# The first stage of a two-block transformer kernel: weights of the modulation added up by whole rows, rows turned ahead of them, the affine step on two engines

## The chip, the cores and the metric

The kernel runs on 1 core of one Trainium2 chip. The metric is the device time of one execution in microseconds (us), taken as the median of several runs. Engines are named as the profile names them: PE (matrix products and transposes), DVE (VectorE), ACT (ScalarE), POOL (GpSimd), SP (SyncE, which here only issues the weight loads).

## The reference, cut to what matters

Two blocks of two layers each over x of 256 rows and 1024 columns, in fp32. The change lies in the entry of the layers of the first block, `hybrid_layer`, where a vector `c` of 1024 numbers modulates the rows:

```python
mod = silu(c) @ w_ada[l] + b_ada[l]        # 1024 x 3072; thirds: shift, scale, gate
u = rms_norm(x, norm_g[l]) * (1 + scale) + shift
proj = u @ w_in[l]                          # z, qb, kb, vb, gates ...
...
x = x + gate * (out @ w_out[l])
```

Everything behind it (attention of three kinds, the feed-forward parts of the second block) is untouched.

## The kernel before, in words

**Weights.** All weights come through one stream. `plan` is a list of chunks of 512 KB or less. SP (`sp`, L2169 to L2178) loads them in the order of `plan` into six buffers `raw`; the load of chunk c waits until chunk c-6 has been used up. A chunk of an ordinary weight is split by ACT into a high part `wh` and by DVE into a remainder `wl` (`split` in both engines), and every product on PE is three matmuls: high by high, high by low, low by high. The chunks of `w_ada` take another way: DVE multiplies each row of 512 columns by one number of silu(c) per partition and adds it to an accumulator `acc` of 512 columns (`weigh`, L1335 to L1352). Such a chunk is two row blocks of 512 columns (kq of 4), so one tile of 512 columns takes four chunks, one multiplication and seven multiply-adds. Then `turn_row` lets PE add over the partitions with a column of ones (four matmuls of 128 columns), and DVE adds `b_ada` into `mod`.

**The start of the program.** PE, ACT, DVE and POOL each follow a list written out by hand; a wait holds all that is behind it on its engine. ACT issues the loads of the identity, of eight short vectors (`rows`, c first), of the constants and of x, in this order, and only then computes the tanh of silu(c), which needs its table loaded. POOL issues ten loads of vectors spread over all partitions (`bc`), the loads of the relative bias and the positions, and twelve tiny loads (`cg`), before its first power, which makes 1/sqrt of the mean square. DVE adds up the tiles (0,0), (0,2), (0,1), (0,3) of `w_ada` of layer 0, sixteen chunks in all. After ten chunks comes `rows_norm`: ACT squares the rows of x, POOL gives the factor, DVE scales them into `xn`. PE turns `xn` into columns only after the last tile of `w_ada` has been turned, since its list has them in that order.

**The affine step** (DVE L1620 to L1636, ACT L1004 to L1014). For each of the eight column blocks of 256 numbers: DVE scales and shifts the turned block out of PSUM into `xtmp` (one of the two halves of `dg`), ACT rounds it into `xt_h`, DVE subtracts for `xt_l`. Behind the eight blocks the first product z begins (`gemm`, chunks of 416 columns), and each engine then splits the chunks that are due: the first six chunks behind the sixteen are w_in, w_in, w_ada, w_in, w_ada, w_in. Layer 1 has the same step with its squares, factor, scaling and turning all behind the end of layer 0.

The names to follow are `first_tiles`, `ada`, `turn_row`, `rows_norm`, `weigh`, `to_xt(("x", l) ...)`, `xtmp` and `rot` (the next of PSUM banks 4 to 6).

Of the kernel before, what the change touches and what calls it, by code (L numbers as in the profile page):

```python
# [246 lines left out]
def build(nc, d, out, ctx):  # L247
# [47 lines left out]
    xtmp = [dg[:, 0:256], dg[:, 256:512]]  # L295
# [74 lines left out]
    first_tiles = [(0, j) for j in (0, 2, 1, 3)]  # L370
    side_tiles = {(0, 0): [(1, 0), (1, 1), (1, 2), (0, 4), (0, 5)], (0, 1): [(1, 3)], (1, 0): [(1, 4), (1, 5)], (1, 1): []}
    ada_tiles = first_tiles + [x for k in sorted(side_tiles) for x in side_tiles[k]]
    ada_no = {x: i for i, x in enumerate(ada_tiles)}

    def chunk_view(buf, c):
        kk, n = plan[c][1:3]
        return buf[:, 0:kk * n].rearrange("p (k n) -> p k n", n=n)

# [57 lines left out]
    def pe(e):  # L436
# [68 lines left out]
        def to_xt(s, src, nch, ready, by="xl"):  # L505

            for c in range(0, nch, 2):
                m = min(2, nch - c)
                b = rot(by, s, c + m - 1)
# [77 lines left out]
        def ada(tiles):  # L587
            for i, (l, j) in enumerate(tiles):
                wv = d["w_ada"][l].rearrange("(c p) n -> p c n", p=128)
                for kq in range(4):  # L590
                    if len(plan) == c_no[0]:
                        plan.append((wv[:, 2 * kq:2 * kq + 2, j * 512:j * 512 + 512], 2, 512, None, None, (l, j, kq)))
# [9 lines left out]
        def turn_row(l, j):  # L602
# [5 lines left out]
            w.wait_ge(*at("cst"))  # L608
            for f in range(4):
                last = mm(b[:, f:f + 1], acc[ada_no[l, j] % 2][:, f * 128:f * 128 + 128], ones_col, True, True)  # L610
            last.then_inc(*up("turn", l, j))

# [7 lines left out]
        first = ada(first_tiles)  # L620
        for _ in range(5):
            next(first)
# [3 lines left out]
        for _ in range(15):  # L626
            next(first)

        ps, pts = Ring(pb1), Ring(pt1)
        for l in range(NL):  # L630
            win = d["w_in"][l]
            to_xt(("x", l), lambda c, t: xn[:, t, c * 128:c * 128 + 128], 8, lambda c, t: [("xn", l, t)], by="xm")
# [168 lines left out]
    def act(e):  # L801
# [183 lines left out]
        first = ada(first_tiles)  # L985
        for _ in range(5):
            next(first)
        e.dma_start(mq[0:32, 0, 0:512], d["consts"][0:32, C_OH:C_END]).then_inc(*landed("oh"))
        rot()

        def rows_norm(l, ready):
            for t in range(2):
                w.wait_ge(*at(*ready(t)))
                old_read(XT)
                ac_(xn[:, t, :], h[:, t, :], ACT.Square,
                    accum_out=stat(1, "rn", l, t)).then_inc(*up("rsq", l, t))

        for _ in range(7):
            next(first)
# [293 lines left out]
    def dve(e):  # L1293
# [325 lines left out]
        for l in range(NL):  # L1619
# [3 lines left out]
            if l:  # L1623
                rows_norm(l)
# [609 lines left out]
```

## Time and profile before

| what | us |
|---|---|
| median of 3 runs (1692.60 to 1696.33) | 1695.83 |
| the profiled execution, its own time | 1694.23 |
| span of the profiled execution | 1692.4 |
| mean granted clock of TensorE | 0.988 |

The time of an execution is 1.8 us more than the span between its first and last instruction. A time of a row is counted from the start of the span. The number after x is how often a group was executed. A timeline's row gives the start and the time on the engine, for one instruction or several alike, and in brackets how long the engine stood idle before it and what ended that. A row of ACTq, SPq or POOL with DMA_DIRECT2D is the issue of a load, not its transfer.

### The profile page before, as it was taken

Reading aid. Unit: us, or ns where it says so; the run is one execution under the profiler, and the core shown is the slowest. Engines: PE = TensorE matmul, PEld = TensorE weight load, DVE = VectorE, ACT = ScalarE, POOL = GpSimd, SP = SyncE. Lnnn points to the kernel's source line nnn. Section 1 sums busy time; section 2 is a strip of 40 time slices with the busy share of each in tenths; the row PEclk is TensorE's granted clock in tenths of the full one; section 3 lists DMA queues with packets and bytes.
Section 4 is the critical chain, followed back from the end, with each engine's and each line's share of the span. In section 5 each row is a group of like instructions: output and inputs, shape, how many; then the busy total and the mean of one; then the engine's idle time right before and its main releaser. Section 6 shows DMA issues by size and latency. Waiting matters only on the chain.

```text
span 1692.4 us, 21793 instructions
## 1 busy us (share of the span) xinstructions
PE 1600.2 (95%) x7796; PEld 1318.4 (78%) x7796; DVE 1067.8 (63%) x1792; ACT 855.9 (51%) x1487; POOL 123.9 (7%) x157
## 2 busy tenths in 40 slices
PE   1679989999999999999999999999999999999998
PEld 1567778778888778878788887888878787788886
DVE  5778577666565646567666556565555567675653
ACT  0346536645444565555454445444455655464442
POOL 3011002100000200002100000000020001200000
PEclk9989989999999999999999999999999999999999
DMA  9565257435555664455565556555582454656552
GB/s 286 199 233 191 74 188 237 132 113 185 188 183 192 160 188 120 136 150 156 187 208 170 194 188 191 186 176 193 174 222 79 130 174 125 205 187 191 178 190 75
DMA packets 155336, 293.27 MB, mean 173 GB/s; under 512 B 10214, under 2 KB 23316, under 8 KB 155228
## 3 DMA queue, kind: packets, MB, share of 16 engines
q1 hardware_dynamic: 149312, 276.60, 50.7%
q0 software_dynamic: 4800, 12.29, 3.1%
q10 hardware_dynamic: 1116, 2.99, 0.5%
q8 instruction: 62, 1.02, 0.2%
q14 instruction: 46, 0.38, 0.1%
HBM read 290.77 MB, written 1.06 MB: 172 GB/s over the span
## 4 chain that ended last, share of the span: by engine, by line
PE 79%; DVE 8%; DMA 5%; ACT 3%; issue 2%; POOL 1%; SPq 0%; DVEq 0%; POOLq 0%; ACTq 0%
PE pb L444 75%; PE pb L448 4%; DMA raw<-in_w_in 3%; DVE wl L1312 2%; DVE acc L1309 1%; DMA raw<-in_w_ada 1%; POOL st L2074 1%; ACT wh L814 1%; DVE xt_l L1309 1%; ACT xt_h L814 1%; DVE dg L1306 0%; DVE h L1309 0%; ACT pb L814 0%; DVE xt_l L1312 0%; DVE pb L1315 0%
## 5 line engine op out<-in xcount | busy, mean ns | idle before, releaser
L814 ACT ACTIVATE wh<-raw 128x1024 fp32r<-128x1024 f32 (+1 forms) x484 | 505.9, 1051 | 454.0 <-PE pb L444 391.5
L1312 DVE TENSOR_TENSOR wl<-raw,wh 128x1024 fp32r<-128x1024 f32 (+1 forms) x484 | 581.4, 1219 | 208.7 <-ACT wh L814 204.6
L444 PE MATMUL pb<-wh,xt_h 128*128 128x512 f32 (+2 forms) x1536 | 593.0, 386 | 12.0 <-ACT wh L814 9.9
L444 PE MATMUL pb<-wl,xt_h 128*128 128x512 f32 (+2 forms) x1536 | 584.8, 381 | 11.9 <-DVE wl L1312 11.8
L444 PE MATMUL pb<-wh,xt_l 128*128 128x512 f32 (+2 forms) x1536 | 585.8, 381 | 1.9 <-DVE xt_l L1309 1.7
L444 PEld LDWEIGHTS pb<-wh,xt_h 128*128 128x128 f32 x1536 | 291.8, 190 | 68.4 <-ACT xt_h L814 10.8
L444 PEld LDWEIGHTS pb<-wl,xt_h 128*128 128x128 f32 x1536 | 292.0, 190 | 64.0 <-DVE wl L1312 13.7
L444 PEld LDWEIGHTS pb<-wh,xt_l 128*128 128x128 f32 x1536 | 291.4, 190 | 62.1 <-DVE xt_l L1309 8.5
L444 PE MATMUL pb<-wh,big_h 128*128 128x512 f32 x352 | 138.7, 394 | 0.0
L444 PE MATMUL pb<-wl,big_h 128*128 128x512 f32 x352 | 138.6, 394 | 0.0
L2074 POOL TENSOR_TENSOR st<-st,cols 128x1 f32<-128x1 f32 (+2 forms) x56 | 53.0, 952 | 1146.6 <-DVE st L1309 759.4
L444 PE MATMUL pb<-wh,big_l 128*128 128x512 f32 x352 | 136.7, 388 | 0.0
L444 PEld LDWEIGHTS pb<-wh,big_h 128*128 128x128 f32 x352 | 66.1, 188 | 15.1
L444 PEld LDWEIGHTS pb<-wh,big_l 128*128 128x128 f32 x352 | 66.1, 188 | 14.8
L444 PEld LDWEIGHTS pb<-wl,big_h 128*128 128x128 f32 x352 | 66.2, 188 | 13.0
L814 ACT ACTIVATE p<-p,st 128x256 f32<-128x256 f32 x96 | 48.1, 502 | 50.6 <-DVE st L1315 50.5
L1309 DVE SCALAR_TENSOR_TENSOR sgt<-ti,pb 128x512 f32<-128x512 f32 (+1 forms) x48 | 30.8, 643 | 59.8 <-ACT ti L814 59.4
L1309 DVE SCALAR_TENSOR_TENSOR hid<-pb,few,sgt 128x512 f32<-128x512 f32 (+1 forms) x48 | 33.9, 707 | 54.4 <-PE pb L444 54.4
L1309 DVE SCALAR_TENSOR_TENSOR acc<-raw,st,acc 128x512 f32<-128x512 f32 x84 | 63.0, 750 | 8.0 <-DMA raw<-in_w_ada 5.1
L814 ACT ACTIVATE pt<-pb 128x512 f32<-128x512 f32 (+1 forms) x80 | 40.3, 504 | 36.1 <-PE pb L448 36.1
L444 PE MATMUL pb<-mkt,mqt 64*128 64x256 f32 x192 | 53.0, 402 | 0.0
L814 ACT ACTIVATE big_h<-pb 128x512 fp32r<-128x512 f32 x44 | 24.2, 596 | 47.9 <-PE pb L448 47.9
(205 smaller groups left out, 1478.0 us busy)
## 6 DMA issues: line engine op xcount, KB each, us to landing
raw<-in_ffn_w_gu SPq DMA_DIRECT2D x176, 512.0 KB, 4.5
raw<-in_w_in SPq DMA_DIRECT2D x148, 512.0 KB, 4.3
raw<-in_ffn_w_down SPq DMA_DIRECT2D x88, 512.0 KB, 3.7
raw<-in_w_ada SPq DMA_DIRECT2D x48, 512.0 KB, 5.5
raw<-in_w_out SPq DMA_DIRECT2D x32, 512.0 KB, 4.3
raw<-in_w_branch SPq DMA_DIRECT2D x24, 512.0 KB, 3.6
raw<-in_w_in SPq DMA_DIRECT2D x8, 416.0 KB, 4.0
G<-in_na_rpb POOLq DMA_DIRECT2D x32, 96.0 KB, 8.5
```

The costliest lines, as they stand in the source:

```text
L444: return e.matmul(o, a, b, start=start, stop=stop)
L448: return e.transpose(o, a, ident[0:n, 0:n])
L814: return e.activation(o, a, func, **kw)
L1309: return e.scalar_tensor_tensor(out=o, in0=a, scalar=s, in1=b, op0=op0, op1=op1)
L1312: return e.tensor_tensor(o, a, b, op)
L2074: e.tensor_tensor(stat(n, "rs", *name), v, halves.to_broadcast([128, n]) if n > 1 else halves, ALU.pow).then_inc(*up("rs", *name))
```

## The change

It does this:

- `w_ada` of layer 0, columns 0 to 2047, comes as sixteen chunks of one row block by 1024 columns in place of two by 512 (`first_ada`), and is added up in two accumulators of 1024 columns (`first_acc`, in `mkv`) by `weigh_row`: one instruction for each chunk, but two halves for the last of each eight.
- ACT's loads come in the order identity, c, x; then a tanh of one column of the identity, then the tanh of c; the other seven short vectors, the constants and the one-hot rows follow behind it.
- POOL's loads of `bc` and `cg` move behind its first two powers (`vectors`).
- The squares are taken in halves of 512 columns; for layer 1 the first halves inside the last product of layer 0. Layer 0's rows are scaled by ACT, layer 1's first half of the rows by DVE and the second by ACT.
- PE turns the rows ahead of the last two tiles of `w_ada`, into banks 2, 3, 7 and one of the rotating ones.
- The affine factor `ac` is made in two halves. DVE scales and shifts blocks 0, 1, 4, 5 and ACT blocks 2, 3, 6, 7, out of four buffers; ACT still rounds and DVE still subtracts all of them. In layer 0 the splitting of the first six chunks stands between the blocks.

```diff
-    xtmp = [dg[:, 0:256], dg[:, 256:512]]
+    xtmp = [dg[:, 0:256], dg[:, 256:512], z0[:, 0, 0:256], z0[:, 1, 0:256]]
...
-    first_tiles = [(0, j) for j in (0, 2, 1, 3)]
+    first_acc = [mkv[:, 0, :], mkv[:, 1, :]]
...
+        def first_ada(j):
+
+            wv = d["w_ada"][0].rearrange("(c p) n -> p c n", p=128)
+            for kx in range(8):
+                if len(plan) == c_no[0]:
+                    plan.append((wv[:, kx:kx + 1, j * 512:j * 512 + 1024], 1, 1024, None, None,
+                                 ("first", j, kx) if kx < 7 else ("acc", 0, j + 1, 7)))
+                c_no[0] += 1
...
+        turn_row(0, 0)
+        turn_row(0, 1)
+        first_ada(2)
...
+            to_xt(("x", l), lambda c, t: xn[:, t, c * 128:c * 128 + 128], 8,
+                  lambda c, t: [("xnv" if l > t else "xn", l, t)], by="xh")
+            if l == 0:
+                turn_row(0, 2)
+                turn_row(0, 3)
```

ACT, its start and its affine step:

```diff
-        for name, r0, n in rows_in:
-            e.dma_start(rows[r0:r0 + n, :], d[name].rearrange("l (c p) -> (l c) p", p=128)).then_inc(
-                *landed("c" if name == "c" else "rows"))
-        e.dma_start(cst[:, 128:], d["consts"][:, 128:C_OH]).then_inc(*landed("cst"))
+        for name, r0, n in rows_in[:1]:
+            e.dma_start(rows[r0:r0 + n, :], d[name].rearrange("l (c p) -> (l c) p", p=128)).then_inc(*landed("c"))
         e.dma_start(h[:, :, :], d["x"].rearrange("b (t p) n -> p (b t) n", p=128)).then_inc(*landed("x"))
         rot()
+        w.wait_ge(*at("id"))
+        ac_(stat(1, "table"), ident[:, 0:1], ACT.Tanh)
         w.wait_ge(*at("ccol"))
         ac_(stat(8, "c_t"), cols[:, 0:8], ACT.Tanh, scale=0.5).then_inc(*up("ctanh"))
+        for name, r0, n in rows_in[1:]:
+            e.dma_start(rows[r0:r0 + n, :], d[name].rearrange("l (c p) -> (l c) p", p=128)).then_inc(*landed("rows"))
+        e.dma_start(cst[:, 128:], d["consts"][:, 128:C_OH]).then_inc(*landed("cst"))
+        e.dma_start(mq[0:32, 0, 0:512], d["consts"][0:32, C_OH:C_END]).then_inc(*landed("oh"))
...
+        for m in (0, 512):
+            rows_squares(0, m, lambda t: ("x",))
+        rows_scale(0, 0)
+        rows_scale(0, 1)
...
+            for c in (2, 6):
+                part = turned(c)
+                next(part)
+                upper(c - 2)
+                next(part)
+                upper(c - 1)
+                if l == 0:
+                    split(stream.lead(1 if c == 2 else 2))
+                upper(c)
+                upper(c + 1)
+                if l == 0 and c == 2:
+                    split(stream.lead(2))
```

DVE, its start and its affine step:

```diff
+            if kx < 7:
+                stt(a, v[:, :], weight, a, ALU.mult, ALU.add).then_inc(*up("first", j, kx))
+                return
+            for i in range(2):
+                o = a[:, i * 512:i * 512 + 512]
+                stt(o, v[:, i * 512:i * 512 + 512], weight, o, ALU.mult, ALU.add).then_inc(*up("acc", 0, j + i, 7))
...
+        split(stream.lead(8))
         b = rot()
         w.wait_ge(*at("rtr"))
         e.tensor_copy(cols[:, 8:126], b[:, 8:126]).then_inc(*up("cols"))
...
+        split(stream.lead(3))
+        turn_row(0, 0)
+        turn_row(0, 1)
+        rows_half(0)
+        rows_var(0)
+        split(stream.lead(5))
...
+                split(stream.lead(1))
+                turn_row(0, 2)
+                affine(0)
+            for c in (0, 4):
+                b = x_banks[c // 2]
+                w.wait_ge(*at("tr", ("x", l), c))
+                w.wait_ge(*at("ac", l, c // 4))
                 for j in range(2):
+                    if c or l:
+                        w.wait_ge(*at("xl", ("x", l if c else 0), j if c else 4 + j))
+                    ts(xtmp[j], b[:, 256 * j:256 * j + 256], ac[l][:, c + j:c + j + 1], mod[:, l, c + j:c + j + 1],
                        ALU.mult, ALU.add).then_inc(*up("xm", ("x", l), c + j))
+                if l == 0 and c == 0:
+                    turn_row(0, 3)
+                    affine(1)
+                lower(c)
+                lower(c + 1)
+                if l == 0:
+                    split(stream.lead(1 if c == 0 else 2))
+                if c:
+                    lower(6)
+                    lower(7)
+                else:
+                    lower(2)
+                    lower(3)
+                    if l == 0:
+                        split(stream.lead(2))
```

POOL:

```diff
         for l in range(NL):
             for t in range(2):
                 rstd(1, "rn", l, t)
+            if l == 0:
+                vectors()
             for t in range(2):
                 rstd(1, "zq", l, t)
```

## Rows read from the trace of the kernel before

**Rows 1.** The page: busy time of each engine over the span.

```profile
PE 1600.2 (95%) x7796; PEld 1318.4 (78%) x7796; DVE 1067.8 (63%) x1792; ACT 855.9 (51%) x1487; POOL 123.9 (7%) x157
```

**Rows 2.** Chain that ended last, from 0 to 110 us: start, length, what.

```profile
3.78 21.64 DMA raw<-in_w_ada
...
44.90 1.84 PE pb L444 x8
```

**Rows 3.** Timeline of the first 35 us: silu(c), x, the first weights, the factor.

```profile
5.00 0.24 PE L448 MATMUL pb<-cst,rows 8*128 8x8 f32 x1 [5.00 <-DMA rows<-in_c]
...
7.98 1.28 ACT L814 ACT_TABLE_LOAD   x1 [7.98 <-issue]
...
9.92 0.49 DVE L1306 TENSOR_SCALAR acc<-raw,st 128x512 f32<-128x512 f32 x1
...
22.52 0.49 DVE L1306 TENSOR_SCALAR acc<-raw,st 128x512 f32<-128x512 f32 x1 [2.81 <-DMA raw<-in_w_ada]
...
24.14 1.06 ACT L814 ACTIVATE ob<-h 128x1024 f32<-128x1024 f32 x1 [14.65 <-DMA h<-in_x]
...
33.38 1.39 POOL L2074 TENSOR_TENSOR st<-st,cols 128x1 f32<-128x1 f32 x2 [18.26 <-DVE st L1306]
```

**Rows 4.** Stretches of 5 us: busy (instructions) by engine, PEclk, DMA share, GB/s.

```profile
0.00:5.00 5.00, 0.00 (x0) 0.03 (x1) 0.00 (x0) 0.00 (x0) 3.96 (x11) 1.00 0.59 184
5.00:10.00 5.00, 0.24 (x1) 0.15 (x1) 0.58 (x4) 1.49 (x2) 4.71 (x12) 1.00 1.05 256
10.00:15.00 5.00, 0.47 (x1) 0.18 (x1) 4.17 (x6) 0.00 (x0) 5.00 (x10) 1.00 0.88 153
...
25.00:30.00 5.00, 0.00 (x0) 0.00 (x0) 4.24 (x6) 1.32 (x4) 0.00 (x0) 1.00 1.05 388
```

**Rows 5.** Groups of the first 60 us by form: busy, mean ns.

```profile
L1309 DVE SCALAR_TENSOR_TENSOR acc<-raw,st,acc 128x512 f32<-128x512 f32 x28 | 21.0, 751 | 6.6 <-DMA raw<-in_w_ada 5.1
...
L2101 POOL DMA_DIRECT2D cg<-in_moba_k_g x4 | 2.3, 574 | 0.0
```

**Rows 6.** Tile ob, whole span: min/median/max ns.

```profile
L1309 DVE SCALAR_TENSOR_TENSOR ob<-ob,sg x4: 1215/1217/1218, 201.2 to 356.3; 128x1024 f32<-128x1024 f32 x4
```

**Rows 7.** Timeline, 44 to 77 us: last tile, turning, affine step, z.

```profile
46.60 2.80 PE L448 MATMUL pb<-cst,ob 128*128 128x128 f32 x12
...
46.98 0.17 DVE L1309 SCALAR_TENSOR_TENSOR ac<-mod,cols 128x8 f32<-128x8 f32 x1
...
57.28 0.54 DVE L1306 TENSOR_SCALAR dg<-pb,ac,mod 128x256 f32<-128x256 f32 x1
57.86 0.42 ACT L814 ACTIVATE xt_h<-dg 128x256 fp32r<-128x256 f32 x1 [0.95 <-DVE dg L1306]
...
58.30 0.42 DVE L1312 TENSOR_TENSOR xt_l<-dg,xt_h 128x256 fp32r<-128x256 f32 x1 [0.48 <-ACT xt_h L814]
```

**Rows 8.** DVE's timeline, 64 to 77 us: the chunks ahead of z's sums.

```profile
64.54 1.02 DVE L1312 TENSOR_TENSOR wl<-raw,wh 128x832 fp32r<-128x832 f32 x1
...
71.77 0.49 DVE L1306 TENSOR_SCALAR acc<-raw,st 128x512 f32<-128x512 f32 x1 [0.84 <-DMA raw<-in_w_ada]
...
74.23 1.23 DVE L1312 TENSOR_TENSOR wl<-raw,wh 128x1024 fp32r<-128x1024 f32 x1 [1.18 <-ACT wh L814]
76.70 0.61 DVE L1438 TENSOR_REDUCE st<-th 128x1 f32<-128x256 f32 x2 [1.25 <-ACT th L814]
```

**Rows 9.** Chain that ended last, 227 to 248 us: layer 1's affine step.

```profile
229.98 1.16 ACT ob L814 x2
...
233.24 0.92 PE pb L448 x3
...
244.77 0.42 DVE xt_l L1312
...
247.37 9.27 PE pb L444 x35
```

**Rows 10.** A stretch behind the first stage, same columns as rows 4.

```profile
100.00:120.00 20.00, 15.41 (x53) 12.70 (x54) 15.41 (x29) 7.55 (x14) 4.25 (x3) 0.66 0.48 159
```

More of the change, by code:

```diff
@@ L508, in to_xt @@
                 m = min(2, nch - c)
-                b = rot(by, s, c + m - 1)
+                if s == ("x", 0) and first_bank_of(c):
+                    b = open_bank(first_bank_of(c), (by, s, c + m - 1))
+                else:
+                    b = rot(by, s, c + m - 1)
                 for j in range(m):
@@ L619, in pe @@
         tr(b[:, 0:8], rows[0:8, :]).then_inc(*up("ctr"))
-        first = ada(first_tiles)
-        for _ in range(5):
-            next(first)
+        first_ada(0)
         b = rot("cols")
@@ L994, in rows_norm, with rows_scale @@
                 old_read(XT)
[L995 to L999, printed above, removed]
-        rows_norm(0, lambda t: ("x",))
-        for _ in range(8):
-            next(first)
+                ac_(xn[:, t, m:m + 512], h[:, t, m:m + 512], ACT.Square,
+                    accum_out=stat(1, "rn", l, t, m)).then_inc(*up("rsq", l, t, m))
+        def rows_scale(l, t):
+            w.wait_ge(*at("rs", "rn", l, t))
+            ac_(xn[:, t, :], h[:, t, :], scale=stat(1, "rs", "rn", l, t)).then_inc(*up("xn", l, t))
+        for m in (0, 512):
+            rows_squares(0, m, lambda t: ("x",))
+        rows_scale(0, 0)
+        rows_scale(0, 1)
         ps, pts, pt_read = Ring(pb1), Ring(pt1), {}
@@ L1555, in dve @@
         e.tensor_copy(cols[:, 8:126], b[:, 8:126]).then_inc(*up("cols"))
-        for c in stream.lead(5):
-            weigh(c)
-        for _ in range(7):
-            next(first)
-        rows_norm(0)
-        for c in stream.lead(6):
-            weigh(c)
-        for _ in range(8):
-            next(first)
+        split(stream.lead(3))
+        turn_row(0, 0)
+        turn_row(0, 1)
+        rows_half(0)
+        rows_var(0)
+        split(stream.lead(5))
         angi = ang[:, 4, :].bitcast(I32)
@@ L1620, in dve, with affine @@
             g8 = cols[:, row_of["norm_g"] + l * 8:row_of["norm_g"] + l * 8 + 8]
-            w.wait_ge(*at("mod", l, 3))
-            stt(ac[l][:, :], mod[:, l, 8:16], 1.0, g8, ALU.add, ALU.mult).then_inc(*up("ac", l))
-            if l:
-                rows_norm(l)
-            for c in range(0, 8, 2):
-                b = rot()
+            def affine(half):
+                m = slice(4 * half, 4 * half + 4)
+                w.wait_ge(*at("cols"))
+                w.wait_ge(*at("mod", l, 2 + half))
+                stt(ac[l][:, m], mod[:, l, 8 + 4 * half:12 + 4 * half], 1.0, g8[:, m], ALU.add, ALU.mult).then_inc(
+                    *up("ac", l, half))
@@ new lines, in lower @@
+            def lower(c):
+                w.wait_ge(*at("xh", ("x", l), c))
+                old_read(XT)
+                tt(xt_l[:, c, :], xtmp[c % 4], xt_h[:, c, :].bitcast(F), ALU.subtract).then_inc(*up("xl", ("x", l), c))
+            if l:
+                affine(0)
+                affine(1)
+                rows_var(l)
+                w.wait_ge(*at("rs", "rn", l, 0))
+                ts(xn[:, 0, :], h[:, 0, :], stat(1, "rs", "rn", l, 0), None, ALU.mult, None).then_inc(
+                    *up("xnv", l, 0))
+                x_banks = [rot() for c in range(0, 8, 2)]
+            else:
+                x_banks = [banks[first_bank_of(c)] if first_bank_of(c) else rot() for c in range(0, 8, 2)]
+                split(stream.lead(1))
+                turn_row(0, 2)
+                affine(0)
```

135 lines of the change are left out of this document (81 added, 54 removed).

## The prediction

> **What bounds the kernel now.** The page comes first: PE is busy 95% of the span, DVE 63%, ACT 51% [rows 1]. So a change at the start can only give back the time in which PE is not yet at work, and the two places where it stands still again. The second view is the chain of waits over the first 110 us. It begins with a load of `w_ada` that was issued at 3.78 and landed 21.64 us later, then runs through DVE's multiply-adds to PE's four matmuls that turn the last tile at 44.90 [rows 2]. The timeline says what made that up. c is there at 5.00, but ACT is still issuing loads and loads its table at 7.98, so DVE's first `w_ada` instruction comes at 9.92; DVE then waits for chunks (2.81 us before the fifth); x lands at 24.14; POOL's two powers end at 34.77 [rows 3]. The stretches show why the loads are late: 256 and 153 GB/s between 5 and 15 us, though the DMA share is 1.05 and 0.88, against 388 GB/s from 25 to 30 us [rows 4]. These are the 10 us in which the small loads of POOL and ACT run beside the weights. From 25 us on DVE is the bound: 28 multiply-adds at 0.751 us [rows 5]. The third piece is the affine step. It starts when `ac` is made at 46.98 and ends when `xt_l` of the last block is there at 58.72 [rows 7], eight rounds of DVE, ACT, DVE in turn. z's first product stands behind it, and the six raw buffers are full meanwhile, so no load runs. The loads that follow come in a burst, DVE waits for them again, and z's sums begin at 76.70 [rows 8]. I measure the first stage by that instant.
>
> **Silu(c).** The table load takes 1.28 us [rows 3]. After the change it can start when the identity and c are there, at 5.0: 6.3, two Tanh and two small DVE steps make 7.2 for the first `w_ada` instruction in place of 9.92 (table to first use was 9.92 - 7.98 = 1.94, and one more small Tanh). Gain 2.7 us, but worth little by itself, since the loads come next.
>
> **The loads up to the last `w_ada` chunk.** 8.39 MB of `w_ada`, 1.05 of x, 0.76 of constants make 10.2 MB. At 388 GB/s [rows 4] they take 26.3 us. The stream's start I read from the first 5 us: 184 GB/s there is 0.92 MB, 2.4 us of a full stream, so it begins at 2.6. With 1.6 us for the small loads that stay early (short vectors, positions, bias), the last chunk lands at 30.5 and the eleventh, five chunks of 1.35 us earlier, at 23.7. What leaves this stretch are `bc` and `cg`: between 5 and 15 us the shortfall against 388 GB/s is 0.66 and 1.18 MB, 4.7 us of a full stream. That is what they cost at most wherever they go.
>
> **DVE's work there.** One 128x1024 multiply-add with two tensors takes 1.217 us [rows 6] where two of 512 took 1.50 [rows 5]. The sixteen chunks are 2 multiplications (0.98 at most each, twice the 0.49 of rows 3), 12 of 1.22 and 4 of 0.75, with 0.06 us between them 20.5 us in place of 24.6. With a first instruction at 7.2 DVE could be done at 29 with no wait, so now loads and DVE bound it nearly alike. The eleventh chunk is added up at 23.7 + 1.28 = 25.0. Two `mod` rows and four tiny steps for the variance bring 26.0. From there two paths run. DVE: four chunks of 1.28 and the last in two halves, 1.6: 32.7 (it was 44.8). The rows: two powers 1.39, two scalings on ACT of 1.06 [rows 3], sixteen transposes at 2.80/12 = 0.23 [rows 7], 3.7: 33.2. This second path is the later one. It is followed by PE's turning of one tile, 1.84 [rows 2], and `mod` and `ac`, 0.4: the first half of `ac` stands at **35.5**, against 47.15 [rows 7]. Gain 11.6 us.
>
> **The affine step with the six chunks.** From `ac` to the end of the sixth chunk's `wl` the kernel takes 65.56 - 47.15 = 18.4 us [rows 7, 8]. Afterwards DVE has four scalings of 0.54, eight subtractions of 0.42, three splits of 1.02 (the first lies ahead of `ac`), two `w_ada` chunks of 1.3 and 1.5 and a small rest of 0.3: 11.8. ACT has four scalings, eight roundings of 0.42 and four splits: about 9. I follow both lists row by row and find one wait of 1 us, DVE for ACT's split of the second chunk. So 12.8 us. Gain 5.6.
>
> **Behind it.** From there to z's sums DVE took 11.2 us, of which 0.84, 1.18 and 1.25 were waits for loads or for what follows from loads [rows 8]. The six chunks free their buffers from 36 us on rather than in one burst at the end, so the next loads are there in time; three `w_ada` chunks and three splits are left, 8.7 us. Gain 2.5. Z's sums begin at 35.5 + 12.8 + 8.7 = 57.0 in place of 76.7, **19.7 us** in all. What follows is a rigid chain of the same instructions, and I let it move whole.
>
> **Layer 1.** Half of the squares goes to the time when ACT waits for PE; of the 1.16 us of squares in the chain about 0.5 stays off. Scaling half of the rows on ACT (1.06) rather than DVE gives back 0.3 of it. From the turned rows to the last `xt_l` it was 245.19 - 234.16 = 11.0 us [rows 9]. With two engines my row by row count gives 7.2, bounded by eight ACT roundings and four ACT scalings. The fourth chunk of z is split behind it, so PE's stretch that began at 247.37 begins about 4 us earlier. Gain 4.0. Bounds: 2 (PE had other blocks to go through meanwhile) and 5.
>
> **The moved loads.** After POOL's powers, at 27.4, its 22 issues of about 0.57 us [rows 5] run to 40. They then share the stream with the first six chunks, in which there was no small load before. The bounds are nothing, if they fall in the time when buffers are full anyway, and the whole 4.7 us. DVE's list has the split of the first chunk ahead of `mod`, so a late chunk would stop the affine step. The chunk is due at 32 us and the heavy part of the shortfall came 4 to 9 us behind the first issue; I take 1.0.
>
> [...]
>
> **Sum.** 19.7 + 4.0 - 1.0 = 22.7 us. The profiled execution took 1694.23, so 1671.5; the median of the runs is 1.6 us above it, so **1673** as a median.
>
> **Rivals.**
> - *The moved loads stop the first weight chunks*: 3 to 5.5 us more than I took, a gain of 14 to 19, so 1677 to 1682. For it: x landed only at 24.14 beside them [rows 3]. Against: the buffers of these chunks are loaded up to 10 us ahead. Chance 0.2.
> - *DVE and the loads go better*: the rows reach PE before the last tile, the loads run at 388 from the start, and layer 1 gives its 5. Gain 26 to 31, 1665 to 1670. Chance 0.15.
> - *The gain is given back behind the stage*: the next stages are short of PE work, and PE is granted 0.66 of its clock from 100 to 120 us, which is 15.4 us of work in 20 [rows 10]. If the shifted pattern brings a second such stretch with PE in the chain, it costs half of about 10 us; and waits for `w_in` may not move along. Gain 6 to 14, 1682 to 1690. Chance 0.08.
> - *The tanh of the identity does not bring the table forward, and x is late all the same*: the rows reach PE some 5 us later, gain 17. Chance 0.04; its time lies in the first rival's.
> - *POOL becomes the bound, and the kernel slower*: the powers of z now stand behind 22 issues, wanted at 57. POOL has 30 us for them, 1.35 us each. Slower than before it would be only from 2.6 us each on, (30 + 23 + 4)/22; the price is then 22 us for each us more per issue. Rows show 0.57. Chance 0.02.
>
> A mechanism for that rival is on the page *SBUF — State Buffer* of the Trainium skill, section "SBUF: two separate sides": POOL can't write the descriptors of its loads while DVE runs in a two-port mode. No run here shows it.
>
> **How the numbers follow.** The forecast (gain 19 to 26, 1669.5 to 1676.5) has 0.51. The range of 1664 to 1684 takes in the first two rivals and the upper edge of the third. A run of this kernel can be told from no change from about 0.2%, 3.4 us. All cases but the last are faster by more than that: faster 0.96, within 0.2% 0.02, slower 0.02.
>
> **What would show it.** In the changed profile: first `w_ada` instruction on DVE near 7.2; x landed before 10; 128x1024 multiply-adds of 1.22; over 350 GB/s from 5 to 25; first `ac` near 35.5; last `xt_l` near 48; z's sums near 57; POOL's issues from 27 to 40. In layer 1, from the squares to PE's fourth chunk 4 us less. The forecast is wrong if the first `ac` comes after 40, if DVE waits over 3 us for ACT's split of the first chunks, or if the stage ends at 57 and the whole is less than 15 us shorter.

## The result and the profile after

The changed kernel takes 1672.56 us as a median (1671.04 to 1673.14, 4 runs), the kernel before 1694.21 (1691.30 to 1696.33, 4 runs): a ratio of 0.987, with a 95% interval of 0.985 to 0.989. That is 21.7 us less; 22.7 were forecast, and 1673. The page shows that no engine does less: the busy times stand as before [rows 1], in a shorter span.

```profile
span 1670.4 us, 21803 instructions
...
PE 1600.3 (96%) x7796; PEld 1319.4 (79%) x7796; DVE 1058.5 (63%) x1773; ACT 863.7 (52%) x1507; POOL 124.0 (7%) x157
```

Next the timeline of the changed kernel up to the first `ac`, which answers to rows 3.

```profile
1.79 0.40 ACTq L1002 DMA_DIRECT2D h<-in_x  x1
...
2.23 1.28 ACT L838 ACT_TABLE_LOAD   x1 [2.23 <-issue]
...
6.30 0.75 DVE L1372 TENSOR_SCALAR mkv<-raw,st 128x1024 f32<-128x1024 f32 x1
...
13.04 0.63 ACT L838 ACTIVATE ob<-h 128x512 f32<-128x512 f32 x1 [7.17 <-DMA h<-in_x]
...
25.89 6.98 DVE L1375 SCALAR_TENSOR_TENSOR mkv<-raw,st,mkv 128x1024 f32<-128x1024 f32 x6
25.91 1.68 POOL L2195 TENSOR_TENSOR st<-st,cols 128x1 f32<-128x1 f32 x2 [22.82 <-DVE st L1375]
...
32.35 3.54 PE L448 MATMUL pb<-cst,mkv 128*128 128x1 f32 x16
...
34.42 0.16 DVE L1375 SCALAR_TENSOR_TENSOR ac<-mod,cols 128x4 f32<-128x4 f32 x1
```

The first `w_ada` instruction comes at 6.30 in place of 9.92, x lands at 13.04 in place of 24.14, the first `ac` is made at 34.42 in place of 46.98. The stretches of the changed kernel, with the columns of rows 4:

```profile
10.00:15.00 5.00, 0.00 (x0) 0.00 (x0) 3.40 (x3) 1.96 (x7) 0.00 (x0) 1.00 1.03 401
15.00:20.00 5.00, 0.47 (x1) 0.18 (x1) 2.85 (x3) 0.60 (x2) 0.00 (x0) 1.00 1.03 392
20.00:25.00 5.00, 3.58 (x16) 3.49 (x16) 4.67 (x7) 0.00 (x0) 0.00 (x0) 1.00 1.03 410
25.00:30.00 5.00, 1.65 (x7) 1.36 (x8) 4.69 (x10) 2.26 (x2) 4.09 (x7) 1.00 1.02 405
30.00:35.00 5.00, 4.93 (x24) 4.56 (x22) 4.26 (x7) 1.21 (x2) 4.71 (x11) 1.00 1.14 303
35.00:40.00 5.00, 5.00 (x17) 4.42 (x17) 4.38 (x11) 2.82 (x7) 4.47 (x9) 1.00 0.90 181
```

Where the kernel before moved 153 GB/s (10 to 15 us, [rows 4]) this one moves 401. The hole is not gone: with POOL's 22 loads (`bc` and `cg`) it has gone to 30 to 40 us. What that does behind the first `ac` the chain of waits of the changed kernel shows:

```profile
32.89 12.85 DMA raw<-in_w_in
45.76 0.91 ACT wh L838
...
49.87 5.84 DMA raw<-in_w_in
55.73 1.06 ACT wh L838
```

From 32.89 to 56.79 it is two loads, 18.7 us, with short pieces of work on ACT and DVE behind each. ACT's timeline has the waits for two of the first six chunks behind `w_ada`'s sixteen, the fourth and the sixth:

```profile
40.62 0.90 ACT L838 ACTIVATE wh<-raw 128x832 fp32r<-128x832 f32 x1 [2.77 <-DMA raw<-in_w_in]
...
45.76 0.90 ACT L838 ACTIVATE wh<-raw 128x832 fp32r<-128x832 f32 x1 [1.52 <-DMA raw<-in_w_in]
```

DVE's timeline ends the stage:

```profile
57.94 0.61 DVE L1525 TENSOR_REDUCE st<-th 128x1 f32<-128x256 f32 x2 [1.24 <-ACT th L838]
```

z's sums begin at 57.94 in place of 76.70 [rows 8], 18.8 us earlier. I follow this gain by landmarks that both kernels have, each the start of the first such instruction:

| landmark, us | before | after | gain |
|---|---|---|---|
| z's sums, layer 0 | 76.70 | 57.94 | 18.8 |
| first `h` of the last product of layer 0 | 216.56 | 197.84 | 18.7 |
| z's sums, layer 1 | 253.20 | 230.05 | 23.2 |
| POOL's first power of the second block | 391.84 | 369.46 | 22.4 |
| end of the span | 1692.4 | 1670.4 | 22.0 |

So layer 0's part moves whole through the 140 us behind it, layer 1 adds 4.4, and 1.1 are lost in the rest. That it moves whole to 0.1 us is in part luck: from z's sums to the first `h` it is 139.9 us here and 137.7 to 141.4 in the experiments below that leave this stretch as it is.

### The profile page after: what moved, and what is told of

Same layout as the page of the kernel before. It is cut to its first block, busy times and chain, and to the rows that moved or that the text cites. A ratio compares the mean times of both kernels' runs of the same rounds, so it can differ in the third digit from the quotient of the medians.

```text
span 1670.4 us, 21803 instructions
## 1 busy us (share of the span) xinstructions
PE 1600.3 (96%) x7796; PEld 1319.4 (79%) x7796; DVE 1058.5 (63%) x1773; ACT 863.7 (52%) x1507; POOL 124.0 (7%) x157
## 2 busy tenths in 40 slices
DMA packets 153288, 293.27 MB, mean 176 GB/s; under 512 B 10214, under 2 KB 23316, under 8 KB 153180
## 4 chain that ended last, share of the span: by engine, by line
PE 82%; DVE 7%; DMA 5%; ACT 3%; issue 2%; POOL 1%; SPq 0%; DVEq 0%; POOLq 0%; ACTq 0%
PE pb L448 77%; PE pb L452 4%; DMA raw<-in_w_in 4%; DVE wl L1378 2%; DMA raw<-in_w_ada 1%; POOL st L2195 1%; ACT wh L838 1%; DVE xt_l L1375 1%; DVE mkv L1375 1%; DVE h L1375 0%; DVE acc L1375 0%; ACT pb L838 0%; DMA raw<-in_mla_w_ukv 0%; DVE pb L1381 0%; ACT ti L838 0%
## 5 line engine op out<-in xcount | busy, mean ns | idle before, releaser
L2279 POOL TENSOR_TENSOR G<-G,mg 128x512 f32<-128x512 f32 x16 | 24.2, 1521 | 263.8 <-DVE mg L1375 263.3
```

The source lines that it names most:

```text
L2279: e.tensor_tensor(m, m, mg[mg_at(n, n0, t)][:, :], ALU.add).then_inc(*up("mrg", g, t))
```

## The experiments

Each is an edit of the changed kernel. A single run gives one time; here its landmarks say more, since the same instructions come out up to 3 us apart in two places behind the first 100 us. One lies ahead of the first `h` (see the rows turned ahead). The other lies from 276 to 317 us: four of the profiled executions below (1675.82, 1676.99, 1677.13 and 1679.54 us) lose 3.0 us there against the changed kernel, at a mean granted clock of TensorE of 0.88, where the changed kernel and the eight others have 0.96. No edit touches that stretch, and PE is busy for 38.4 of its 41 us in the four and 38.1 in the changed kernel. What sets the clock there is not known. So a single time of 1675 us or more says little of an edit here.

**Where the small loads lie.** First the 22 loads back to the head of POOL's list:

```diff
+        vectors()
         e.memset(cols[:, 126:128], -0.5).then_inc(*up("half"))
...
-            if l == 0:
-                vectors()
```

> The changed kernel with the 22 loads of bc and cg put back to the head of POOL's list. Theory (moving them is worth something, but not the 4.7 us): the weights of the first stage come late again (under 300 GB/s from 5 to 15 us), the first half of ac stands 3 to 4 us later than the 34.6 of the changed kernel, at 38; but the first six chunks behind the stage come without small loads beside them, so ACT's waits of 2.8 and 1.5 us for them go, and z's sums begin at 58 to 60 against 57.9. Time 1673 to 1675. Rival A (their place is worth the whole 4.7 us): z's sums at 62 to 63, 1677. Rival B (the moved loads stop the first chunks and cost more than they gave): z's sums before 57, 1670 to 1671.

Measured: 1677.55 us median (1675.42 to 1681.69, 4 runs; ratio to before 0.991, 0.989 to 0.993). The rows of the profiled execution (first stretches, then DVE's timeline):

```profile
10.00:15.00 5.00, 0.00 (x0) 0.00 (x0) 1.28 (x1) 0.00 (x0) 5.00 (x12) 1.00 0.95 190
15.00:20.00 5.00, 0.00 (x0) 0.00 (x0) 1.46 (x2) 1.21 (x4) 0.32 (x1) 1.00 0.92 286
...
35.00:40.00 5.00, 4.30 (x20) 3.86 (x19) 4.69 (x6) 1.55 (x2) 0.00 (x0) 1.00 1.05 396
```

```profile
17.81 1.28 DVE L1375 SCALAR_TENSOR_TENSOR mkv<-raw,st,mkv 128x1024 f32<-128x1024 f32 x1 [5.92 <-DMA raw<-in_w_ada]
...
41.31 0.16 DVE L1375 SCALAR_TENSOR_TENSOR ac<-mod,cols 128x4 f32<-128x4 f32 x1
...
61.14 0.61 DVE L1525 TENSOR_REDUCE st<-th 128x1 f32<-128x256 f32 x2 [0.50 <-ACT th L838]
```

The first `ac` comes 6.9 us later than in the changed kernel, more than even rival A had; z's sums at 61.14 are 3.2 later, and the span is 1673.6, again 3.2 more. ACT waits for neither the fourth nor the sixth chunk. So the moved loads won 6.9 us ahead of `ac` and gave 3.7 of them back behind it; net 3.2 in this trace. The median says 5.0, with a spread of its own runs of 6 us. The theory had the mechanism and both signs, but its numbers were too small: z's sums lie between its 58 to 60 and rival A's 62 to 63, and the median of 1677.55 is rival A's 1677.

The other side of it: none of the 22 in the first 60 us. The loads of `cg` go behind the load of `gv`, those of `bc` behind the powers of kb:

```diff
+        def small_vectors():
             e.memset(cg[:, :], 1.0).then_inc(*up("cgone"))
...
-            if l == 0:
-                vectors()
...
                     *landed("gv"))
+                small_vectors()
             for nm in ("qb", "kb"):
                 for t in range(2):
                     rstd(8, nm, l, t)
+            if l == 0:
+                vectors()
```

> The changed kernel with the loads of cg behind the load of gv and those of bc behind the powers of kb, so that none of the 22 runs in the first 58 us. Theory (in the changed kernel they make the first chunks behind the stage late): from 30 to 40 us over 350 GB/s until the buffers are full, no wait of ACT over 1 us for w_in between 35 and 47 us, z's sums at 54 to 55.5 in place of 57.9, time 1669 to 1670.5. Rival (those chunks were early enough, or the loads take the same time away where they now stand): z's sums at 57 or later, or earlier but the time still within 1 us of 1672.6.

Measured: z's sums at 54.91, 3.0 us earlier than in the changed kernel, as the theory said; and the time is 1677.19 median (1674.06 to 1679.54, 4 runs), 4.6 *more*. The trace, of the slowest of the four runs, shows where it goes, when each instruction of DVE is held against the same one of the changed kernel. The lead of 3.0 us falls to 1.3 by 77 us, behind the twelve loads of `cg` at 62 to 68 us (in the next experiment, which leaves `cg` early, it falls from 3.4 to 2.7). Between 102 and 116 us it turns into a lag of 2.9. The ten loads of `bc`, issued from 97.76 to 103.3 us, then run beside the weights of the MLA projections. ACT's timeline of this kernel, where the changed one has a wait of 6.87 at this place:

```profile
108.79 0.63 ACT L838 ACTIVATE wh<-raw 128x512 fp32r<-128x512 f32 x1 [10.82 <-DMA raw<-in_mla_w_ukv]
...
114.83 1.06 ACT L838 ACTIVATE wh<-raw 128x1024 fp32r<-128x1024 f32 x1 [2.06 <-DMA raw<-in_w_in]
```

The first h of the last product comes at 202.43 against 197.84: from `gp` (107.20 against 107.52) to there it is 95.2 us, where the changed kernel has 90.3 and no other trace over 91.8. The ten loads cost 4.4 us at this place. Of the 7.3 us by which this execution's span is longer, another 3.0 are those from 276 to 317 us. The theory had nothing of this. The rival had its first half, loads that take the time away where they now stand, but not that they take more.

Of the ten `bc` loads eight are wanted only in the second block. They can go where the stream is idle, behind the load of `b_ada` at 156 us:

```diff
-            for name, a0, n in bc_in:
+            for name, a0, n in bc_in[:2]:
...
-                    *landed("bc"))
+                    *landed("bcm"))
...
                 *landed("bgate", l))
+            if l == 0:
+                for name, a0, n in bc_in[2:]:
+                    e.dma_start(bc[:, a0:a0 + n], bass.AP(tensor=d[name].tensor, offset=0, ap=[[0, 128], [1, n]])
+                                ).then_inc(*landed("bc"))
```

> The changed kernel with cg and the two bc loads of the first block where they are, and the eight others of bc, wanted in the second block alone, behind the load of b_ada of layer 0 at 156 us, where the loads leave the stream at 90 to 157 GB/s. Theory (the small loads cost by their time on the engines of the DMA, so what lies where the stream is idle is free): 35 to 40 us over 220 GB/s, ACT's two waits for the fourth and sixth chunk 1.5 us shorter together, z's sums at 55.5 to 56.8, time 1670 to 1671.3. Rival (the cg loads of 4 bytes are the costly ones, or the place at 156 us costs as much): z's sums after 57.2, or earlier and the time 1672 or more.

Measured: 1670.30 us median (1668.53 to 1671.16, 4 runs; ratio to before 0.985, 0.984 to 0.987), z's sums at 54.52. Stretches and ACT's timeline:

```profile
30.00:35.00 5.00, 4.93 (x24) 4.56 (x23) 4.33 (x7) 0.90 (x1) 5.00 (x11) 1.00 0.91 308
35.00:40.00 5.00, 5.00 (x17) 4.44 (x18) 4.28 (x12) 4.49 (x9) 0.80 (x2) 1.00 0.94 323
...
155.00:170.00 15.00, 14.68 (x90) 12.86 (x89) 6.95 (x29) 9.23 (x32) 3.52 (x7) 1.00 0.76 142
```

```profile
31.88 0.90 ACT L838 ACTIVATE wh<-raw 128x832 fp32r<-128x832 f32 x1 [2.54 <-DMA raw<-in_w_in]
...
38.32 0.89 ACT L838 ACTIVATE wh<-raw 128x832 fp32r<-128x832 f32 x1
...
43.22 0.89 ACT L838 ACTIVATE wh<-raw 128x832 fp32r<-128x832 f32 x1
...
46.67 1.06 ACT L838 ACTIVATE wh<-raw 128x1024 fp32r<-128x1024 f32 x1 [1.00 <-DMA raw<-in_w_in]
```

The waits of 2.77 and 1.52 us for the fourth and sixth chunk (38.32 and 43.22 here) are gone, and 323 GB/s run from 35 to 40 us where it was 181. The fourteen loads that stayed, `cg` and two of `bc`, cost next to nothing there: z's sums come as early as with none of the 22 (54.91). The cost of the eight loads at 156 us is a share of 0.76 in a stretch that had 0.32, with PE busy 14.68 of 15 us as before. z's sums are 3.4 us earlier, the first power of the second block (366.80) 2.7, the span 1.9. Its median is 2.3 us below the changed kernel's. That does not prove a gain in time: the two intervals against before overlap, the two were not timed side by side, and the kernel with the rows turned later (below), which has all 22 loads where the changed kernel has them, has a median of 1670.52 and its first power of the second block at 367.49. Shown is the gain of 3.4 us at z's sums, where every trace with the 22 loads in the changed kernel's place has 57.6 to 58.4.

**The tanh of the identity.**

```diff
-        w.wait_ge(*at("id"))
-        ac_(stat(1, "table"), ident[:, 0:1], ACT.Tanh)
```

> The changed kernel without the tanh of a column of the identity. Theory (the table load is placed ahead of the wait by itself, it needs only ACT to be free): the table load still at 2.2 us, the first w_ada instruction on DVE at 6.3 as now, the time within 1 us of 1672.6. Rival (the extra tanh brings it forward): the table load at 5.7 or later, the first w_ada instruction at 7.6; since the loads are the bound then, z's sums at most 1.3 us later.

Measured: 1671.31 us (one run). The table load is at 2.23 here too, the first `w_ada` instruction at 6.29. What brought the table forward is that only three loads stand ahead of it on ACT in place of eleven; the extra tanh does nothing. The theory held.

**Runs of 2 KB or 4 KB.**

```diff
-                    plan.append((wv[:, kx:kx + 1, j * 512:j * 512 + 1024], 1, 1024, None, None,
+                    plan.append((wv[:, kx, j * 512:j * 512 + 1024].rearrange("p (g n) -> p g n", g=2), 1, 1024, None, None,
```

> The changed kernel with each of the sixteen 1024-column chunks of w_ada loaded as two runs of 2 KB per partition in place of one of 4 KB (the same bytes and the same instructions on DVE). Theory (the longer runs are why 10 to 30 us show 392 to 410 GB/s where the kernel before never had over 393): 375 to 390 GB/s there, the last w_ada row on DVE 0.5 to 1 us later. Rival (the rate is higher because the small loads are away): 400 GB/s and more as in the changed kernel and no difference in time.

Measured: 1671.69 us (one run), 409 GB/s from 10 to 15 us. It tells nothing on the question: the page counts 153288 packets, as many as for the changed kernel and 2048 fewer than before, so the two runs were joined into one of 4 KB again. It stands as a second run of the changed kernel (z's sums 58.09).

**The rows turned ahead.** The sixteen transposes go behind the turning of the last two tiles again:

```diff
+            if l == 0:
+                turn_row(0, 2)
+                turn_row(0, 3)
             to_xt(("x", l), lambda c, t: xn[:, t, c * 128:c * 128 + 128], 8,
                   lambda c, t: [("xnv" if l > t else "xn", l, t)], by="xh")
-            if l == 0:
-                turn_row(0, 2)
-                turn_row(0, 3)
```

> The changed kernel, in layer 0 with the sixteen transposes of the rows behind the turning of the last two tiles of w_ada, as before the change. Theory (behind the first ac the stage is set by when the fourth and sixth chunk land, at 40.6 and 45.8 us, not by the engines): the first scaled block on DVE comes 2 us later, at 36.7 in place of 34.7, ACT's wait of 2.8 us for the fourth chunk shrinks to about 0.8, and z's sums begin within 0.7 us of 57.9. Rival (the engines set the pace): the 2 us stay, z's sums at 59.5 to 60, time 1674.5.

Measured: 1675.82 us, but z's sums at 57.70. DVE's timeline shows the 2 us and where they are lost again:

```profile
34.19 0.16 DVE L1377 SCALAR_TENSOR_TENSOR ac<-mod,cols 128x4 f32<-128x4 f32 x1
36.65 0.99 DVE L1374 TENSOR_SCALAR dg<-pb,ac,mod 128x256 f32<-128x256 f32 x2 [2.31 <-PE pb L452]
```

ACT then has no wait for the fourth and the sixth chunk at all. The time spoke for the rival and the landmark for the theory, so the same kernel was timed again:

> The same kernel as e5_turn_after, timed in rounds. Theory (turning the rows ahead is worth nothing where loads set the pace; the 3.6 us of the single look came from a stretch at the lower granted clock at 140 to 155 us): median within 1.5 us of 1672.6. Rival (it is worth its 2 us or more somewhere behind): 1674.5 or more in all rounds.

Measured: 1670.52 us median (1669.55 to 1671.35, 4 runs; ratio to before 0.986, 0.984 to 0.988), z's sums at 58.02. That is 2.1 us below the 1672.6 of the theory, on the other side from the rival. Turning the rows ahead brings z's sums no earlier. The first run lost its time elsewhere: z's sums are the same within 0.3 us in both, but from 140 to 155 us the first run of this very kernel had PE at a mean granted clock of 0.77, the second at 0.89. First the one, then the other:

```profile
140.00:155.00 15.00, 10.90 (x56) 9.23 (x55) 10.65 (x31) 7.33 (x18) 3.27 (x2) 0.77 0.30 94
```

```profile
140.00:155.00 15.00, 11.28 (x68) 9.86 (x69) 10.88 (x27) 10.18 (x21) 3.74 (x3) 0.89 0.34 107
```

and its first h came at 198.96 against 195.76. That is 3.2 of the 6.3 us between the two executions; another 2.9 lie from 276 to 317 us, with 0.88 against 0.96. A clock of 0.77 from 140 to 155 us does not make a slow run by itself: the next experiment has it too, at 1672.99 us.

**The second engine, layer 0 and layer 1.** DVE scales and shifts all eight blocks, in pairs as before but into four buffers; ACT only rounds. Once for layer 0, once for layer 1, with the one condition changed:

```diff
+                if l == 0:
+                    w.wait_ge(*at("tr", ("x", l), c + 2))
+                    for j in range(2):
...
+                        ts(xtmp[2 + j], x_banks[c // 2 + 1][:, 256 * j:256 * j + 256],
+                           ac[l][:, c + 2 + j:c + 3 + j], mod[:, l, c + 2 + j:c + 3 + j],
+                           ALU.mult, ALU.add).then_inc(*up("xm", ("x", l), c + 2 + j))
                 if c:
                     lower(6)
```

> The changed kernel, in layer 0 with all eight blocks scaled and shifted by DVE (four more instructions of 0.54 us on DVE, four fewer on ACT). Theory (the loads set the pace there): DVE's waits of 1.4, 0.55 and 0.34 us in the step take up most of the 2.2 us; z's sums 0 to 1.2 us later than 57.9. Rival (this is what the 5 us of the step come from, my forecast's view): 2.5 to 4 us later, time 1675 or more.

Measured: 1672.99 us (one run), z's sums at 58.13, 0.2 later. The theory held: loads set that pace. It was not tried with the small loads out of the way.

> The changed kernel, in layer 1 with all eight blocks scaled and shifted by DVE. Theory (no load is waited for there, and most of layer 1's 4.4 us come from the second engine): from the first h of the last product of layer 0 to layer 1's z sums 34.5 to 36 us in place of 32.2, time 1675 to 1676.5. Rival (most of it comes from the squares, the scaling by ACT, four buffers in place of two and the other order): under 33.7 us, time under 1674.

Measured: 1672.17 us (one run). From the first h to layer 1's z sums 31.97 us (197.26 to 229.23), against 32.21 in the changed kernel. The theory fell; up to z's sums the second engine is worth nothing in layer 1 either. DVE's timeline shows what remains without it:

```profile
214.76 0.99 DVE L1375 TENSOR_SCALAR dg<-pb,ac,mod 128x256 f32<-128x256 f32 x2 [2.21 <-PE pb L452]
215.79 0.88 DVE L1381 TENSOR_TENSOR xt_l<-dg,xt_h 128x256 fp32r<-128x256 f32 x2
216.59 0.99 DVE L1375 TENSOR_SCALAR z<-pb,ac,mod 128x256 f32<-128x256 f32 x2
217.61 0.88 DVE L1381 TENSOR_TENSOR xt_l<-z,xt_h 128x256 fp32r<-128x256 f32 x2
...
221.25 0.88 DVE L1381 TENSOR_TENSOR xt_l<-z,xt_h 128x256 fp32r<-128x256 f32 x2
...
229.23 0.61 DVE L1528 TENSOR_REDUCE st<-th 128x1 f32<-128x256 f32 x2
```

No wait is left between them: two scalings are long enough for ACT to round the first block meanwhile. It is 1.82 us for a pair, 0.91 a block, where it was 1.36. The same rows of the changed kernel:

```profile
215.21 0.99 DVE L1372 TENSOR_SCALAR dg<-pb,ac,mod 128x256 f32<-128x256 f32 x2 [2.06 <-PE pb L452]
...
220.89 0.76 DVE L1378 TENSOR_TENSOR xt_l<-z,xt_h 128x256 fp32r<-128x256 f32 x2
...
230.05 0.61 DVE L1525 TENSOR_REDUCE st<-th 128x1 f32<-128x256 f32 x2 [1.42 <-ACT th L838]
```

So the step itself, from the first scaling to the last `xt_l`, takes 6.4 us with two engines and 7.4 with one. The second engine is worth 0.9 us in the step; they are lost ahead of z's sums, where DVE waits 1.42 us for ACT's `th`. To see whether the pairs are what layer 1 won, they were taken away too, and DVE goes block by block in layer 1:

```diff
+            for c in range(8 if l else 0):
+                w.wait_ge(*at("tr", ("x", l), c // 2 * 2))
+                w.wait_ge(*at("ac", l, c // 4))
+                w.wait_ge(*at("xl", ("x", l if c > 3 else 0), c - 4 if c > 3 else c + 4))
+                ts(xtmp[c % 4], x_banks[c // 2][:, 256 * (c % 2):256 * (c % 2) + 256], ac[l][:, c:c + 1],
+                   mod[:, l, c:c + 1], ALU.mult, ALU.add).then_inc(*up("xm", ("x", l), c))
+                lower(c)
```

> The changed kernel, in layer 1 with DVE alone and one block at a time (scale, wait for ACT's rounding, subtract), as before the change. Theory (what layer 1 won is that two blocks are scaled before the first is subtracted, so that ACT's rounding runs beside DVE): the step at 1.36 us a block again in place of 0.91 with one engine in pairs, so from the first h of the last product of layer 0 to layer 1's z sums 35.5 to 36.5 us in place of 32.0 to 32.2. Rival (the squares and the other splits of work made it): under 33.5 us.

Measured: 36.58 us from the first h (195.89) to layer 1's z sums (232.47). The kernel before has 36.64. So with the turn by turn order 4.6 us come back against one engine in pairs, 4.4 against the changed kernel, and the waits with it; the step is 11.0 us long, as before the change:

```profile
213.41 0.55 DVE L1375 TENSOR_SCALAR dg<-pb,ac,mod 128x256 f32<-128x256 f32 x1 [2.21 <-PE pb L452]
214.44 0.42 DVE L1381 TENSOR_TENSOR xt_l<-dg,xt_h 128x256 fp32r<-128x256 f32 x1 [0.48 <-ACT xt_h L838]
```

The time of this single run, 1673.30, shows only part of it; the early landmarks of that execution were 2 us ahead of the changed kernel's.

**The splits between the blocks.** In layer 0 the six chunks are split behind the eight blocks, on both engines:

```diff
-                split(stream.lead(1))
                 turn_row(0, 2)
                 affine(0)
...
-                if l == 0:
-                    split(stream.lead(1 if c == 0 else 2))
...
+            if l == 0:
+                split(stream.lead(6))
```

> The changed kernel, in layer 0 with the splits and additions of the first six chunks behind the eight blocks instead of between them. Theory (the order on the lists is worth more than the second engine, since it frees the buffers early): last xt_l at 42 to 43 us, the next loads issued only from 43 on, z's sums at 60 to 61.5, the time about 2.5 to 3.5 us up, 1675 to 1676. Rival (with the moved small loads in the way the buffers could not have been refilled in time anyhow): z's sums within 0.7 us of 57.9.

Measured: 1676.99 us (one run), z's sums at 58.36, 0.4 later: the rival. SP's timeline shows that it does free the buffers late, as the theory had it (two loads in a row):

```profile
33.09 0.92 SPq L2298 DMA_DIRECT2D raw<-in_w_in  x1
42.04 0.37 SPq L2298 DMA_DIRECT2D raw<-in_w_ada  x1
```

The load at 42.04 and the three behind it (42.96, 44.10, 45.08) go out at 33.89, 38.37, 40.18 and 42.65 in the changed kernel. The same z's sums come out all the same; that it is because the small loads fill just these us is the rival's reading and was not tested by itself. The 4.4 us of its span beyond those 0.4 arise behind z's sums: 3.0 of them are those from 276 to 317 us, 1.5 lie ahead of the first h, where the two executions of one kernel, above, also came apart.

**The width of the additions.**

```diff
             if kx < 7:
-                stt(a, v[:, :], weight, a, ALU.mult, ALU.add).then_inc(*up("first", j, kx))
+                stt(a[:, 0:512], v[:, 0:512], weight, a[:, 0:512], ALU.mult, ALU.add)
+                stt(a[:, 512:1024], v[:, 512:1024], weight, a[:, 512:1024], ALU.mult, ALU.add).then_inc(
+                    *up("first", j, kx))
```

> The changed kernel with each 1024-column instruction of weigh_row as two of 512 columns. Theory (DVE is the bound from the ninth chunk on, the loads before it): the instructions cost 0.28 us more per chunk, the last w_ada row 2 to 3 us later, first ac at 36.5 to 37.5 in place of 34.4; of that the stage behind it, which waits for loads, takes back about half: z's sums at 58.5 to 59.5, time 1673 to 1674.5. Rival (loads bound it all along): ac within 0.5 us of 34.4.

Measured: 1677.13 us (one run, 3.0 of it lost from 276 to 317 us), first `ac` at 35.38, z's sums at 58.19. 1.0 us ahead of `ac`, 0.25 behind it. In its chain of waits the pairs of halves start at 26.34, 27.86 and 29.38, 1.52 apart; in that of the changed kernel the wide ones start at 25.89, 27.29, 28.68, 30.07 and 31.45, 1.39 apart. The wide form is worth 0.13 us a chunk. DVE's timeline has the last ten halves in one group:

```profile
26.34 7.48 DVE L1375 SCALAR_TENSOR_TENSOR mkv<-raw,st,mkv 128x512 f32<-128x512 f32 x10
```

Neither had it: the theory's 0.28 a chunk was too much, and the rival's bound by loads does not hold either.

## Why the prediction was right, and where it was not

**The number.** 1673 forecast, 1672.56 measured; the gain 22.7 and 21.7. By terms: up to z's sums 18.7 forecast (19.7 less the 1.0 for the moved loads) and 18.8 measured, layer 1 4.0 and 4.4, the rest nothing and -1.1. The mechanism of the first stage, loads without small loads beside them and a shorter list on DVE, is what the runs show. But within the stage terms are wrong by up to 2.4 us, with opposite signs, so that the sum is this close is in part luck.

**Silu(c).** 7.2 us forecast, 6.30 measured. The table load did not wait for the identity and c, as I had it: it starts at 2.23, when ACT has issued its third load.

**The loads up to the last chunk.** The forecast took 388 GB/s all along; measured are 318 from 5 to 10 us and 392 to 410 from 10 to 30. x was to land before 10 us and landed at 13.04: I had not worked out how the queues share the stream. It cost nothing, as the squares were done long before POOL was asked (25.91).

**DVE's work.** Here terms were mis-sized: "one 128x1024 multiply-add takes 1.217 us" and 0.06 between them. They took 1.284 and follow at 1.39. The instruction of rows 6 that I took the price from has a constant as its factor; these read theirs from a tile, one for each partition, and such instructions took about 60 ns more (see the last section). The two multiplications took 0.75 and not 0.98. The last `w_ada` row ended at 32.87, forecast 32.7, since DVE had begun earlier. The two paths I had drawn met: PE ended its transposes at 32.28 and turned at once.

**First ac.** 34.58 measured, 35.5 forecast, 47.15 before. Of the 12.6 us, 6.9 are lost again when the small loads alone are put back and 1.0 when the width alone is halved. The rest, 4.7 if the parts add up (earlier silu, x ahead of the constants, the scaling off DVE's list), was not taken apart.

**The affine step.** This is the step that failed in its reasons while its number stood, and that is luck. "Gain 5.6" from the two engines' lists: from `ac` to the sixth chunk's `wl` it is 13.1 us against 12.8 forecast. In the three traces in which ACT waits for none of the chunks behind the first (the 22 loads first, late, and eight of them late) the same stretch takes 11.0 us. So my lists were 1.8 us too long, and 2.1 us of waits that come with the loads, which I had at nothing in this step, made up for it. And with one engine in place of two z's sums move by 0.2 us, with the splits behind by 0.4, with the rows turned later by -0.2 to 0.1. The lists I had summed are not the bound; the fourth and sixth chunk are, which land late because the small loads lie beside them (ACT's waits 2.77 and 1.52 us). Without those loads there z's sums come 3.0 to 3.4 us sooner. What the second engine and the pairs are worth in layer 0 once the loads are out of the way no run shows.

**Behind it.** 8.7 us forecast up to z's sums, 10.2 measured (47.72 to 57.94). I had said that the next loads would be there in time. They are not: 385 to 388 GB/s run from 45 to 60 us, a full stream. In the three traces named above it is 8.4 to 8.9 us, so the term itself was right, and the rest belongs to the moved loads.

**The moved loads.** I took 1.0 us of cost, and 4.7 as what they can cost at most wherever they go. Measured are 3.0 to 3.4 of cost and 6.9 of return ahead of `ac`, the net as forecast within half a us: 3.2 against 3.7. The 4.7 are no upper bound: between all 22 at the head and none in the stage lie 6.2 us of z's sums (61.14 and 54.91). The first rival, the moved loads stopping the first weight chunks, was half right. Its mechanism is in the trace, but they cost 2.0 to 2.4 us more than I took and not its 3 to 5.5.

By the page *DMA: Bandwidth & Descriptors* of the Trainium skill, section "Issuing engines are not separate DMA queues", the DMAs of all engines run on the same 16 DMA engines and interleave there, and issuing them on several engines saves only the time of issuing. The traces agree that they share them: beside POOL's loads the weights slow down, at a DMA share of 0.95. When a load should run the section does not say, and that is what counted here: z's sums are at 61.14 with the 22 loads at the head, at 57.94 behind the first powers, and at 54.5 to 54.9 with the large ones later still.

**Layer 1.** 4.0 forecast, 4.4 measured, and "with two engines my row by row count gives 7.2" was the wrong cause. The step took 6.4 us, but one engine in pairs (7.4) has its z's sums as early; pairs taken away give all of it back. The squares and the scaling, for which I had 0.8 us, brought 0.25: from the first h to the first scaled block it is 17.37 us and was 17.62.

**Slower.** POOL's 22 issues took 12 us as forecast (27.55 to 39.47), and POOL then stood idle for 19.23 us before the powers of z at 58.70. The issues took 0.53 us each beside DVE at work, and 0.57 at the head of the kernel before. By the page *SBUF — State Buffer* of the Trainium skill, section "SBUF: two separate sides", DVE in a two-port mode would have held them up; no row shows such a hold, and none says in which mode DVE ran.

**What stays open.** The 1.1 us lost behind layer 1; why the same instructions from 120 to 200 us come out up to 3 us apart and those from 276 to 317 us 3.0 us; how much of the higher rate comes from 4 KB runs.

## What to carry to other kernels

A small load spread over all partitions costs the weight stream far more than its bytes, and what it costs depends on what the stream carries at that moment: put it where the stream is idle and where its data are wanted late (by its landmarks that is a gain here, by its median not for certain), and read GB/s beside the DMA share to find it. In a step in which two engines hand a block to and fro, begin a second block before the first is taken back; that alone gave in layer 1 what a second pair of hands was thought to give. And where a step is followed by a wait for a load, adding up the engines' lists says nothing about it, right as the sum may look. Take the price of an instruction from one with the same kinds of operands. And when one execution comes out slow, compare landmarks before you blame the edit.

## What the runs showed of the hardware

- 22 loads of 0.73 MB in all took the stream (from 10 us on) from 401 to 190 GB/s for 5 us and from 392 to 286 for the next 5, at DMA shares of 0.95 and 0.92. That is a loss of 1.6 MB in these 10 us. The ten of `bc` beside the MLA weights lengthened a wait from 6.87 to 10.82 us and cost 4.4 us there.
- It is time on the DMA engines that such loads cost, not bytes: in the first 60 us of the changed kernel POOL's queue moved 0.74 MB in 8.8% of the engines' time, SP's 17.19 MB in 77.8%. Packets of 4096 bytes took 489 ns each on average on POOL's queue, where they carry the vectors spread over all partitions, and 168 ns on SP's.
- A single core read weights at 392 to 410 GB/s for 20 us. The page *DMA: Bandwidth & Descriptors* of the Trainium skill, section "Where 436 GB/s comes from", has about 358 as what binds between HBM and SBUF, beside a measurement of its own of 425; the runs here side with the latter. The kernel before had 388 as its best stretch of 5 us in the first 60.
- DVE's instruction on two tensors and a factor (SCALAR_TENSOR_TENSOR) took about 60 ns more where its factor is read from a tile, one for each partition, than where it is a constant: 1284 ns (`mkv<-raw,st,mkv`) and 1217 (`ob<-ob,sg`, [rows 6]) for 1024 columns; 745 to 751 (`h<-yf,st,h`, `ti<-pb,few,ring`, `hid<-pb,few,sgt`) and 683 to 689 (`sg<-th,pb`, `mg<-mg,pb`) for 512. That it adds into one of its own inputs is not what costs: `ti` and `hid` do not.
- The table load of ACT ran ahead of the wait of the instruction that needs it (at 2.23 us, while that instruction starts at 5.09). Without the extra tanh it was at 2.23 as well.
- The same 41 us of instructions took 3.0 us longer in four of thirteen executions that have them in the same place, at a mean granted clock of 0.88 in place of 0.96.
